# First attention: a head's value product in three parts of two key tiles, behind the scores of three items, in place of one block of six

## The reference, cut to what matters

```python
def blocked_attention(q, k, v):                     # q: 512 tokens, 6 heads of 128
    nb = lq // Q_BLOCK                              # four blocks of 128 queries
    scale = dh ** -0.5
    def one_block(qblk):
        s = jnp.einsum('bqhgd,bkhd->bhgqk', qblk, k, preferred_element_type=jnp.float32) * scale
        p = jax.nn.softmax(s, axis=-1).astype(v.dtype)
        return jnp.einsum('bhgqk,bkhd->bqhgd', p, v)
    o = lax.map(one_block, qb)
...
k_all = jnp.concatenate([ck, k], axis=1)            # 256 + 512 = 768 keys
y = concat([ya * silu(a_gate), yb * silu(b_gate)]) @ w_out      # yb is the attention's output
```

## Time and profile before

| | us |
|---|---|
| median of the runs (3) | 2310.51 |
| lowest and highest of them | 2306.3, 2312.8 |
| the profiled execution's own time | 2306.9 |
| its span | 2305.1 |
| mean granted clock of TensorE | 0.937 of full |
| attention: first scores to the start of the pool mixer's matmuls | 243.55 to 347.90 |

### The profile page before, as it was taken

How to read it: one execution, slowest core, us unless ns; L and a number is a source line. 1 busy time by engine, 2 the same in 40 slices (tenths; PEclk the granted TensorE clock), 3 DMA queues, 4 the chain that set the end, 5 groups by cost and what they waited for, 6 DMA issues and landing times.

```text
span 2305.1 us, 26281 instructions
## 1 busy us (share of the span) xinstructions
PE 2071.7 (90%) x9652; PEld 1577.6 (68%) x9652; DVE 1162.4 (50%) x1894; ACT 808.2 (35%) x1358; POOL 99.5 (4%) x105
## 2 busy tenths in 40 slices
PE   6797889899788989988899999998997888999997
PEld 5684446687455557855598888775874578888775
DVE  4565547796676673256465323325235547423323
ACT  2424342443322233225454323224223545423421
POOL 0003000000200000000030000000000012000000
PEclk9898899999899999997799999999996989999998
DMA  7574007576001252310031322222220021232222
GB/s 249 191 283 154 0 0 259 200 280 250 7 7 60 81 212 75 108 37 1 11 119 46 101 91 93 89 91 91 93 89 1 1 74 56 91 103 98 91 79 85
DMA packets 46936, 233.28 MB, mean 101 GB/s; under 512 B 5095, under 2 KB 6631, under 8 KB 29832
## 3 DMA queue, kind: packets, MB, share of 16 engines
q1 hardware_dynamic: 46856, 232.22, 28.6%
HBM read 229.97 MB, written 2.10 MB: 101 GB/s over the span
## 4 chain that ended last, share of the span: by engine, by line
PE 77%; DVE 11%; ACT 5%; issue 3%; DMA 2%; POOL 1%; SPq 0%; DVEq 0%; POOLq 0%; ACTq 0%
PE banks L1797 17%; PE banks L1798 17%; PE banks L1799 17%; PE banks L1991 3%; PE banks L2013 2%; PE banks L1839 2%; PE banks L1927 1%; PE banks L1828 1%; PE banks L1830 1%; PE banks L1829 1%; DMA w_raw<-in_wt 1%; PE banks L2156 1%; PE banks L2167 1%; PE banks L2095 1%; PE banks L2220 1%
## 5 line engine op out<-in xcount | busy, mean ns | idle before, releaser
L1114 DVE TENSOR_TENSOR w_low<-w_raw,w_high 128x1024 fp32r<-128x1024 f32 x220 | 268.9, 1222 | 473.8 <-ACT w_high L485 473.1
L1797 PE MATMUL banks<-h_high,w_high 128*128 128x512 f32 x1208 | 473.0, 392 | 21.4 <-DVE w_low L1114 17.7
L1798 PE MATMUL banks<-h_low,w_high 128*128 128x512 f32 x1208 | 472.4, 391 | 0.0
L1799 PE MATMUL banks<-h_high,w_low 128*128 128x512 f32 x1208 | 472.2, 391 | 0.0
L485 ACT ACTIVATE w_high<-w_raw 128x1024 fp32r<-128x1024 f32 x222 | 233.5, 1052 | 191.3 <-PE banks L1799 158.0
L1797 PEld LDWEIGHTS banks<-h_high,w_high 128*128 128x128 f32 x1208 | 228.2, 189 | 72.8 <-DVE w_low L1114 15.8
L1799 PEld LDWEIGHTS banks<-h_high,w_low 128*128 128x128 f32 x1208 | 228.1, 189 | 47.7
L1798 PEld LDWEIGHTS banks<-h_low,w_high 128*128 128x128 f32 x1208 | 228.0, 189 | 47.1
L1797 PE MATMUL banks<-hidden_high,w_high 128*128 128x512 f32 x512 | 207.8, 406 | 0.0
L1798 PE MATMUL banks<-hidden_low,w_high 128*128 128x512 f32 x512 | 200.0, 391 | 0.0
L1799 PE MATMUL banks<-hidden_high,w_low 128*128 128x512 f32 x512 | 199.7, 390 | 0.0
(11 more groups left out here) (429 smaller groups left out, 3166.8 us busy)
## 6 DMA issues: line engine op xcount, KB each, us to landing
w_raw<-in_wt SPq DMA_DIRECT2D x129, 1024.0 KB, 4.9
mod_raw<-in_wmod SPq DMA_DIRECT2D x144, 512.0 KB, 5.0
cmp_w<-in_cmp_w SPq DMA_DIRECT2D x2, 2048.0 KB, 9.2
x<-in_xT SPq DMA_DIRECT2D x1, 2048.0 KB, 10.5
dft<-in_dft SPq DMA_DIRECT2D x1, 2048.0 KB, 13.4
out_x<-x SPq DMA_DIRECT2D x8, 256.0 KB, 2.0
hy_w<-in_hy_w SPq DMA_DIRECT2D x8, 192.0 KB, 3.3
tab_attn<-in_tab_attn SPq DMA_DIRECT2D x1, 1216.0 KB, 9.9
```

Of the source, the lines that this page charges most:

```text
L1114: v.tensor_tensor(low[:, :, :].rearrange("p k c -> p (k c)"), RAW[b // 2][:, b % 2, :], high[:, :, :].rearrange("p k c -> p (k c)").bitcas ...
L1797: mm(out, high[:, k, :], H[:, kk, :], start=start and k == 0, stop=False)
L1798: mm(out, high[:, k, :], L[:, kk, :], start=False, stop=False)
L1799: last = mm(out, low[:, k, :], H[:, kk, :], start=False, stop=stop and k == KT - 1)
```

## The change

`head_values` gets a list of key tiles. In PE's loop it is called at three of four items, n % 4 = 1, 2 and 3 (from n = 5 on), with the tiles 0 and 1, then 2 and 3, then 4 and 5, instead of once with all six; the head is still (n - 5) // 4. The semaphore `attn_o` is counted up by the last part. Head 5 stays one block of six behind the loop. On DVE a head's gate moves from n = 6, 10, ... to n = 8, 12, ..., and head 4's gate from n = 22 to behind the loop. The following lines are numbered one or more higher from there on. No operation, shape or buffer is added or taken away.

```diff
@@ DVE
-            if n >= 6 and n % 4 == 2:
-                head_gate((n - 6) // 4)
+            if n >= 8 and n % 4 == 0:
+                head_gate((n - 8) // 4)
         normalise(23)
+        head_gate(4)
         head_gate(5)
@@ PE
-        def head_values(h):
+        def head_values(h, parts):
             pe.wait_ge(*when(f"pt.{4 * h + 3}"))
             if h >= 2:
                 pe.wait_ge(*when(f"attn_y.{h - 2}"))
-            for j in range(6):
+            for j in parts:
                 last = mm(bank(6 + h % 2), VT[:, j, ...], PT[h % 2][:, j, :], start=j == 0, stop=j == 5)
-            last.then_inc(*did(f"attn_o.{h}"))
+            if parts[-1] == 5:
+                last.then_inc(*did(f"attn_o.{h}"))
...
-            if n >= 5 and n % 4 == 1:
-                head_values((n - 5) // 4)
+            if n >= 5 and n % 4:
+                head_values((n - 5) // 4, range(2 * (n % 4) - 2, 2 * (n % 4)))
             if n:
                 transpose_probs(n - 1)
         transpose_probs(23)
-        head_values(5)
+        head_values(5, range(6))
```

## The result

| us | before | after |
|---|---|---|
| median of the runs (6 each) | 2306.97 | 2295.57 |
| lowest and highest | 2304.59, 2312.80 | 2294.19, 2299.59 |
| span of the profiled execution | 2305.1 | 2297.8 |

The ratio is 0.995, with a 95% interval from 0.9934 to 0.9965: faster by 11 us, with 8 to 15 in the interval. The profiled execution of the changed kernel (2299.59) was the slowest of its six. A second series of the changed kernel on another occasion gave 0.9964 (0.9947 to 0.998).

The account below looks back on a forecast made before the run. Bound: DVE and ACT's chain for two to three items, PE's value block in the others, never overlaid. Terms 7.8 + 2.7 + 2.2 = 12.7 us off the mean 2309.1 gave 2296.4, range 2290 to 2304.

Parts of the forecast that it names:

- The intervals: Between starts of successive heads' first value parts in the attention: 16.19 to 14.23 us, 1.96 each, 7.8 for four.
- The hand-overs: On PE, from scores into a value part: taken at 0; rival 0.43 late for ten parts, 4.3 us, chance 0.09.
- The gates: DVE's head gates in their new places cost nothing; without its cover head 4's would cost 0.68 us, once.
- The way to item 23's transposes: From the last looped head's first part to item 23's transposes: 10.68 us in place of 13.41, a gain of 2.73.
- The clock at the end: PE's clock stays up for item 23's transposes and head 5's block: 2.16 us more, bounds 0 and 2.16.
- the rival that the clock falls all the same: PE's clock still falls at the attention's end: gain 10.5 us, time 2298.6, chance 0.15.
- The sign of being wrong that I had named: Wrong if first parts came 16 apart, starts within a part's item 4.1 or more, or clock 0.50 in 260 to 330.
- The sum: Intervals 7.8, last stretch 2.7 and clock at the end 2.2: a gain of 12.7 us.
- What lies behind: After the attention, nothing with a clock of its own is late next; what follows starts earlier by the whole gain.
- The slower rival: In the attention loop, shorter, more frequent PE pauses and bank changes lower the clock: a loss of 2.9, 2312, chance 0.03.

Follow-up runs that it names:

- two parts: The values in two parts of three key tiles instead of the change's three parts, gates as in the change: intervals of 15.20 us.
- four items: Against the change, values spread over all four items (2, 1, 2 and 1 key tiles), gates moved: intervals 13.37 us; median 2292.03, ratio 0.9939 to the kernel before.
- second profile: The changed kernel profiled again, no edit: intervals of 14.22 us, last block 5.26 us at clock 1.00.

## Why the prediction was right, point by point

- **The intervals** (forecast 14.23, gain 7.85 for four): 14.23, and 64.77 - 56.90 = 7.87. That PE bounds three items, that the margins on DVE are short but there, and that the next first part still waits for ACT's copy are all in the chain above; two parts and four items came out by the same sums (15.2 and 15.20; 13.3 and 13.37).
- **The hand-overs** (taken at 0, up to 4.3): 0. Scores end and parts start without a gap (263.68 + 0.43 = 264.11).
- **The gates** (0): 0 where they now stand. DVE idles 0.46 us behind the gate in the loop, and head 4's gate ran at 327.65, ahead of 8.60 us in which DVE had nothing to do.
- **The way to item 23's transposes** (13.41 to 10.68, a gain of 2.73): 10.96, a gain of 2.45. I had checked these transposes against DVE's scaling alone. They also wait for ACT's copy of item 22 out of the one pair of banks, and with the third part ahead of item 22's own transposes that copy is the later of the two, by 0.28.
- **The clock at the end** (forecast 2.16, bounds 0 and 2.16): this step failed in the first profile. Item 23's transposes did run at full clock and the copy followed earlier (2.44 to 1.75, 0.69 of it), but the block lost 0.19 in place of winning 1.50, since the fall now came at its very start. In the second profile the forecast was met (5.26). In three of four profiles the rival that the clock falls all the same described the end, and to the chance of 0.15 that it had I would now give more than half. The reason that I gave for the upper bound doesn't hold either: the intervals of the kernel before have no stretch as thin as the one that I expected ahead of the block, about 1.5 us of work in 3.3. The thinnest 3.56 us in them still have 2.17 us of PE's work:

```profile
269.84:273.40 3.56, 2.17 (x10) 1.29 (x10) 2.10 (x6) 2.32 (x6) 0.00 (x0) 1.00 0.01 2
```

The sign of being wrong that I had named, a clock of 0.50 in 260 to 330, was passed by little: the fall came at 330.19.
- **The sum** at the pool mixer's matmuls: forecast 12.7, measured 10.8 in the first profile (7.87 + 2.45 + 0.69 - 0.19) and 12.5 in the second (87.38 - 74.86).
- **What lies behind** was to come earlier by the whole gain. In the medians it did, nearly: 11.4 us, and 10.5 in the second series. In a single pair of profiles it did not (7.3), by the clock in a stretch that has nothing to do with the change. To place the gain on the mean of all four runs then known (2309.1) and not on the profiled one came out at 2296.4 against 2295.57; the base was 2 too high and the gain 1.3 too large. That the two errors took each other back for the most part is luck; the gain is the better test.
- **Smaller readings**, which change nothing above: of DVE's six waits of "about 4 us each" five are of 4.4 and the first is of 3.0, ahead of the intervals. The transposes behind the first part have had their scaled probabilities for 1.7 us (260.28 to 262.00), not for over 2. The values that a gate in the loop needs had ended 3.0 us before it (269.50 to 272.54), not 2.
- **The slower rival** (a clock that falls in the loop because PE changes banks and pauses more often) has no support: the granted clock is 1.00 in the intervals. Its premise was wrong as well: PE paused three times per interval before (1.17, 0.77 and 0.61 us) and pauses once now (1.02); the 14 short waits behind the first part are DVE's. The page "TensorE: Matmul & The Clock Gate" of the Trainium skill, named there with its section on a second failure mode by queue depth, tells of a kernel with matmuls in BF16. Here they are FP32, and within the intervals this case's traces don't bear that section out for either order: a change of bank at each step, short pauses, and a granted clock of 1.00.

## What to carry to other kernels

Where one engine has a long block once per several turns of a chain that it otherwise waits for, compare the block with the slack of one turn: cut it so that each turn's work on that engine comes close to the chain's length (2.93 here). Each turn then takes the longer of the two, and the interval is their sum: 14.2 us in three parts and 13.4 over four items, where it was 16.2 in one piece. Before that, look for an instruction on the other engines that waits for the end of the block, and move it behind the place where the last piece now ends; left where it was, it took back all of the gain here. Judge a change of half a per cent by the place it is made in, from one fixed row of the trace to another, and the whole by medians, since one execution's clock elsewhere is worth as much as the change: a single time of the kernel before, taken beside the last profiles, was 2297.63, as low as the changed kernel's.

## What the runs showed of the hardware that was not expected

- The same order of work at the attention's end met the lower clock in three of four executions and not in the fourth, with PE busy 1.67 of the 3.56 us ahead of the block in each of them. The cost is 1.7 us when it comes. Of the six profiles of other kernels in which PE was busy 2.53 us or more there, none met it.
- A stretch of the later layer that is the same in all kernels took from 156.8 to 165.6 us in fourteen profiles, at a granted clock of 0.82 (841 PE matmuls in its first 158.4 us) down to 0.74 (782). Within one kernel it varied by 8 us.
- The attention's intervals of the changed kernel are 14.22 or 14.23 us in all four of its profiles.
